# Expert jobs of 96 rows, with the weights held in the array in the up products

## The chip, the cores and the metric

One NeuronCore of a Trainium2 chip runs the whole program in one launch. The metric is device time in microseconds (us), the median of several executions. PE stands for TensorE's matmuls, PEld for its weight loads, DVE for VectorE, ACT for ScalarE, POOL for GpSimd and SP for SyncE, which here only issues transfers.

## The reference

A two-layer transformer over 256 tokens of width 1024, all float32. Each layer has a mixer (four kinds of token mixing, not touched here) and a feed-forward part. In the first layer that part is dense, in the second it is a mixture of eight experts, of which each token takes two:

```python
def swiglu(h, w1, w3, w2):
    return (jax.nn.silu(h @ w1) * (h @ w3)) @ w2

def moe_swiglu(h, w_router, w1, w3, w2):
    logits = (h @ w_router).astype(jnp.float32)
    top_v, top_i = lax.top_k(logits, TOP_K)                      # TOP_K = 2
    gates = jax.nn.softmax(top_v, axis=-1)
    combine = jnp.sum(jax.nn.one_hot(top_i, N_EXPERTS, ...) * gates[..., None], axis=-2)
    for e in range(N_EXPERTS):                                   # 8 experts, width 3584
        out = out + combine[..., e:e + 1] * swiglu(h, w1[e], w3[e], w2[e])
```

So 512 token rows are spread over eight experts. Counted by the reference's router on its own inputs, the experts get 53 to 78 rows each.

## The kernel before

The expert stage works through a list of jobs. A job is one expert and up to C = 128 of its token rows (`C = P`, L46); an expert with more rows than C would get a second job. There are eight jobs here. An expert's 3584 hidden columns are cut into 14 pairs of 256 columns, and each pair has three pieces of weights of 1 MB: two up pieces (w1 and w3 side by side, for the first and the second half of the 1024 inputs) and one down piece. So the stage has 112 pairs and 336 pieces.

SP fetches the pieces into a ring of seven slots (L1110). ACT rounds each piece to float32r (`wh`, L491), DVE takes the remainder (`wl`, L495), and `wh` and `wl` have four buffers each. Every product is made of three matmuls, high by high, high by low and low by high, all of float32r.

In `pe_up` (L402) the token rows are held in the array and the weights stream past them: 12 matmuls of 512 columns for each up piece (L417), 24 for a pair. Token rows then lie on PSUM's partitions, and w1's 256 columns and w3's lie side by side in one bank. ACT takes silu of the first half (L522), and DVE multiplies it with the second (`gate`, L577). The down product needs the hidden columns on partitions, so PE transposes the gated values (`pe_turn_gated`, L424, two transposes at L430), ACT rounds the result (`gh`, L535) and DVE takes the remainder (`gl`, L586). `pe_down` (L433) makes 12 matmuls of 512 columns (L442), again with the token values held in the array.

The order of PE is written out in `pe_steps` (L456): up half 0 of pair m, the transposes of pair m-1, up half 1 of pair m, down of pair m-1. ACT and DVE have their own written order, a round for each pair (L543 and L596): first the split of the gated values of pair m-1, then the up weights of pair m+1, silu and gate of pair m, and the down weights of pair m. Between two jobs PE also transposes the next rows (L854). In the dense layer the same functions hold the weights in the array and stream 256 columns of tokens past them (L420, L446).

Of the kernel before, what the change touches and what calls it, by code (L numbers as in the profile page):

```python
# [45 lines left out]
C = P  # L46
# [113 lines left out]
def program(nc, A, out):  # L160
    ctx = ExitStack()
    with ctx:
# [233 lines left out]
        TURNS = 4  # L396

# [4 lines left out]
        def pe_up(pe, run, m, par, part):  # L402
            stage, buf = run.up(m, part)
            pe.wait_ge(sem("w_split"), stage + 1)
            if part == 0:
                wait(pe, "gated", run.item(m - 1))
            w = [b[:, buf].rearrange("p (k n) -> p k n", n=2 * T) for b in (wh, wl)]
            for item in range(run.parts):
                for kind in range(1 if run.moe else 2):
                    for k in range(4):  # L410
                        for n, (a, b) in enumerate(((0, 0), (0, 1), (1, 0))):
                            x = (xh, xl)[a][:, 4 * part + k]

                            kw = {"start": part == kind == k == n == 0, "stop": part == 1 and k == 3 and n == 2,
                                  "skip_group_check": True}
                            if run.moe:
                                ins = nc.tensor.matmul(up_bank(run, par, 0)[:], x[:, 0:C], w[b][:, k], **kw)  # L417
                            else:
                                at = kind * T + item * P
                                ins = nc.tensor.matmul(up_bank(run, par, item)[:, kind * T:(kind + 1) * T],  # L420
                                                       w[b][:, k, at:at + P], x, **kw)
            ins.then_inc(sem("stage_used"), 1)

        def pe_turn_gated(pe, run, m):  # L424

            if run.moe:
                pe.wait_ge(sem("gated"), run.item(m) + 1)
                pe.wait_ge(sem("g_split"), run.before_pairs + m)
                for a in range(2):
                    ins = nc.tensor.transpose(bank[TURNS][:, a * P:(a + 1) * P], gate[:, 0, a * P:(a + 1) * P], cst("id"))  # L430
                ins.then_inc(sem("g_turned"), 1)

        def pe_down(pe, run, m, last=False, first=False, followed=False):  # L433
            stage, buf = run.down(m, last, followed)
            pe.wait_ge(sem("w_split"), stage + 1)
            pe.wait_ge(sem("g_split"), run.before_pairs + m + 1)
            w = [b[:, buf].rearrange("p (a n) -> p a n", a=2) for b in (wh, wl)]
            for o in range(2 if run.moe else KT):
                for a in range(2):
                    for g, b in ((gh, 0), (gh, 1), (gl, 0)):  # L440
                        if run.moe:
                            ins = nc.tensor.matmul(bank[2 + o][:], g[:, a, 0:C], w[b][:, a, o * 512:(o + 1) * 512],  # L442
                                                   start=first and a == 0 and g is gh and b == 0, stop=False,
                                                   skip_group_check=True)
                        else:
                            ins = nc.tensor.matmul(bank[2 + o // 2][:, o % 2 * T:(o % 2 + 1) * T],  # L446
                                                   w[b][:, a, o * P:(o + 1) * P], g[:, a],
                                                   start=first and o % 2 == a == b == 0 and g is gh, stop=False,
                                                   skip_group_check=True)
                if last and not run.moe and o % 2 and o < KT - 1:  # L450
                    ins.then_inc(sem("acc_ready"), 1)
                if last and run.moe and not followed and o == 0:
                    ins.then_inc(sem("acc_ready"), 1)
            ins.then_inc(sem("stage_used"), 1)

        def pe_steps(pe, run, j=0):  # L456

            def step(m, par, first=False):
                pe_up(pe, run, m, par, 0)
                pe_turn_gated(pe, run, m - 1)  # L460
                pe_up(pe, run, m, par, 1)
                if first and run.moe:
                    wait(pe, "acc_copied", 2 * j)
                pe_down(pe, run, m - 1, first=first)

            n = run.pairs - 1
            if run.moe:
                step(1, 1, True)
                with pe.Fori(0, n // 2) as i:
                    step(2 * i + 2, 0)  # L470
                    step(2 * i + 3, 1)
                return
            step(1, 1, True)
            with pe.Fori(0, (n - 1) // 2) as i:
                step(2 * i + 2, 0)
                step(2 * i + 3, 1)
            if n % 2 == 0:
                step(n, 0)
# [33 lines left out]

        def act_silu(act, run, m, par):
            for item in range(run.parts):
                if not run.moe:
                    act.wait_ge(sem("scaled"), run.item(m) + item + 1)
                    nc.scalar.activation(silu[:, item], silu[:, item], ACT.Silu, bias=cst("zero")
                                         ).then_inc(sem("silu_done"), 1)
                    continue
                act.wait_ge(sem("stage_used"), run.up(m, 1)[0] + 1)  # L520
                wait(act, "gated", run.item(m - 1) + item + 1)
                nc.scalar.activation(silu[:, item], up_bank(run, par, item)[:, 0:T], ACT.Silu, bias=cst("zero")  # L522
                                     ).then_inc(sem("silu_done"), 1)

        def act_gated_high(act, run, m):

            if run.moe:
                act.wait_ge(sem("g_turned"), run.before_pairs - PAIRS_D + m + 1)
                o, i = gh[:, :, 0:C], bank[TURNS][:, 0:2 * C].rearrange("p (a c) -> p a c", c=C)
            else:  # L530
                act.wait_ge(sem("gated"), run.item(m) + 2)
                o, i = gh[:], gate[:]
# [36 lines left out]
        def dve_gate(dve, run, m, par):  # L569
            for item in range(run.parts):  # L570
# [6 lines left out]
                nc.vector.tensor_tensor(gate[:, item], up_bank(run, par, item)[:, T:2 * T], silu[:, item], ALU.mult  # L577
                                        ).then_inc(sem("gated"), 1)

        def dve_gated_low(dve, run, m):  # L580
            dve.wait_ge(sem("g_high"), run.before_pairs + m + 1)
            if run.moe:
                o, i, h = gl[:, :, 0:C], bank[TURNS][:, 0:2 * C].rearrange("p (a c) -> p a c", c=C), gh[:, :, 0:C]
            else:
                o, i, h = gl[:], gate[:], gh[:]
# [10 lines left out]
        def dve_steps(dve, run):  # L596
            up, down = splitter(dve, split_low, run)

            for m in range(1, run.pairs - 1):
                dve_gated_low(dve, run, m - 1)  # L600
                up(m + 1, 0)
                if not run.moe:
                    dve_scale(dve, run, m, m % 2)
                    up(m + 1, 1)
                dve_gate(dve, run, m, m % 2)
                if run.moe:
                    up(m + 1, 1)
# [186 lines left out]
        def placed(tt=slice(0, TT)):  # L794
            return gh[:, tt, C:2 * C]

        def y_part(low, half):
            return (xh, xl)[low][:, 4 * half:4 * half + 4, C:2 * C]

        def acc_half(half):  # L800
            return bank[2 + half][:].rearrange("p (k c) -> p k c", c=C)
# [6 lines left out]
        def pe_moe(pe, mm, turn):  # L808
# [39 lines left out]
            def gather(j):  # L848

                pe.wait_ge(sem("x_loaded"), 16 * j)  # L850
                for half in range(2):
                    for d in range(4):
                        k = 4 * half + d
                        turn(bank[5 + half][:, d * C:(d + 1) * C], xrow[:, k * P:(k + 1) * P],  # L854
                             sig="gathered" if d == 3 else None)
# [11 lines left out]
            with pe.Fori(1, n_jobs) as j:  # L867
                run, nxt = job(j - 1), job(j, True)
                pe_turn_gated(pe, run, last)
# [9 lines left out]
            pe_turn_gated(pe, run, last)  # L879
            pe.wait_ge(sem("sel_built"), 2)  # L880
            for tt in range(TT):
                turn(bank[7][:, tt * P:(tt + 1) * P], sel[:, tt], sig="place_turned" if tt else None)
# [8 lines left out]
        def act_moe(act, copy, f):  # L891
# [9 lines left out]
            def gathered(j):  # L901
                for half in range(2):
                    act.wait_ge(sem("gathered"), 2 * j + half + 1)
                    nc.scalar.activation(xh[:, 4 * half:4 * half + 4, 0:C],
                                         bank[5 + half][:].rearrange("p (k c) -> p k c", c=C), ACT.Copy
                                         ).then_inc(sem("x_high"), 1)

            def acc(j):
                act.wait_ge(sem("stage_used"), job(j).used())
                act.wait_ge(sem("y_stored"), 16 * j + 16)  # L910
                for half in range(2):
                    nc.scalar.copy(yj[:, half * 512:(half + 1) * 512], bank[2 + half][:]).then_inc(sem("acc_copied"), 1)
# [23 lines left out]
            nc.scalar.activation(placed(), bank[7][:, 0:T].rearrange("p (a c) -> p a c", c=C), ACT.Copy).then_inc(sem("last_high"), 1)  # L936
# [13 lines left out]
        def dve_moe(dve, settle, tt_, ts, stt, recip):  # L950
# [44 lines left out]
            def gathered(j):  # L995
                for half in range(2):
                    dve.wait_ge(sem("x_high"), x_before(1, 2) + 2 * j + half + 1)
                    hv = slice(4 * half, 4 * half + 4)
                    nc.vector.tensor_tensor(xl[:, hv, 0:C], bank[5 + half][:].rearrange("p (k c) -> p k c", c=C),
# [3 lines left out]
            for i in range(2):  # L1003
                settle(nc.vector.tensor_tensor(hit[:, i], cst("iota").unsqueeze(1).broadcast_to([P, TT, C]),
# [17 lines left out]
            for i in range(2):  # L1022
                settle(nc.vector.tensor_tensor(hit[:, i], cst("iota").unsqueeze(1).broadcast_to([P, TT, C]),
# [43 lines left out]
        def pool_moe(pool, settle):  # L1067
# [9 lines left out]
            def load(j):  # L1077
                pool.dma_start(xrow[:], job_x[bass.ds(j * C, C), :]).then_inc(sem("x_loaded"), 16)

            def store(j):  # L1080
                pool.wait_ge(sem("acc_copied"), 2 * j + 2)
                pool.dma_start(job_y[bass.ds(j * C, C), :], yj[:]).then_inc(sem("y_stored"), 16)
# [98 lines left out]
        def _(pool):  # L1181
# [17 lines left out]
            for layer in range(DEPTH):  # L1199
# [50 lines left out]
                if layer == 0:  # L1250
                    settle(nc.gpsimd.memset(xrow[:], 0.0))
                    for rows_, sig in ((job_x, "zero_filled"), (job_y, "y_stored")):
                        pool.dma_start(rows_.rearrange("(j p) d -> p j d", p=C),
                                       xrow[:].unsqueeze(1).broadcast_to([P, MAXJOBS, D])).then_inc(sem(sig), 16)
# [1154 lines left out]
```

## Time and profile before

| | us |
|---|---|
| three runs | 1645.98, 1646.78, 1652.68 |
| median | 1646.78 |
| span of the profiled execution | 1645.5 |
| first up product of the experts in that execution | 672.4 |
| last down product done | about 1634 |

The profile is one execution. A page gives busy time by engine, the span in 40 slices, the chain that ended last and the costliest groups of instructions. The trace behind it gives the same for any stretch, and the instructions one by one. A matmul row's own duration is longer than the step to the next one, because matmuls are pipelined: what a stream of them costs is the step from start to start.

### The profile page before, as it was taken

The page shows a single profiled execution, that of the slowest core. Times are in us where ns is not written, and L with a number is a line of the kernel's source. Part 1 is how long each engine was busy: PE and PEld are TensorE (multiplying, and loading weights), DVE is VectorE, ACT ScalarE, POOL GpSimd, SP SyncE. Part 2 cuts the span into 40 slices and gives each one's busy share as a digit, 9 for nine tenths or more (in the row PEclk, how much of TensorE's full clock was granted, in tenths as well). Part 3 has the DMA queues.
Part 4 walks back from the last instruction along what each step waited for, and adds up shares of the span by engine and source line. Part 5 has one row for each costly group of instructions (what it writes and reads, how often), then busy time and mean ns, then how long its engine had stood idle before and what let it go on. Part 6 is the DMA issues. An engine that isn't in the chain of part 4 may idle for free.

```text
span 1645.5 us, 27766 instructions
## 1 busy us (share of the span) xinstructions
PE 1585.1 (96%) x10290; PEld 1363.3 (83%) x10290; DVE 1283.7 (78%) x1252; ACT 1041.8 (63%) x1038; POOL 139.9 (9%) x152
## 2 busy tenths in 40 slices
PE   7999989999899999899999999999999999999997
PEld 7987789999898778788888888888888888888776
DVE  4885556555558656688889889889888888988997
ACT  4634454344354445577777777777777777777675
POOL 1062000000006200100000000000000000001720
PEclk9999999999999999999999999999999999999999
DMA  7429165542252105699999999999999999999992
GB/s 252 159 89 398 55 256 184 186 170 99 80 176 88 40 2 225 247 374 375 382 375 374 389 375 377 382 374 384 378 375 361 399 373 367 395 373 369 398 356 111
DMA packets 68272, 457.56 MB, mean 278 GB/s; under 512 B 7296, under 2 KB 8480, under 8 KB 16752
## 3 DMA queue, kind: packets, MB, share of 16 engines
q1 hardware_dynamic: 59984, 425.80, 67.1%
q0 software_dynamic: 8080, 30.84, 4.9%
q8 instruction: 43, 0.70, 0.2%
q14 instruction: 21, 0.17, 0.0%
q10 hardware_dynamic: 144, 0.05, 0.0%
HBM read 433.07 MB, written 23.59 MB: 278 GB/s over the span
## 4 chain that ended last, share of the span: by engine, by line
PE 54%; issue 3%; DVE 3%; ACT 2%; DVEq 0%; ACTq 0%
PE bank L417 33%; PE bank L442 17%; DVE wl L495 2%; PE bank L430 1%; ACT wh L491 1%; PE bank L738 1%; PE bank L1271 1%; DVE gl L586 0%; PE bank L814 0%; PE bank L1276 0%; PE bank L483 0%; DVE gate L577 0%; ACT wide L1770 0%; ACT oh L728 0%; DVE rstd L2026 0%
## 5 line engine op out<-in xcount | busy, mean ns | idle before, releaser
L495 DVE TENSOR_TENSOR wl<-ring,wh 128x2048 fp32r<-128x2048 f32 x369 | 854.0, 2318 | 157.7 <-ACT wh L491 154.4
L491 ACT ACTIVATE wh<-ring 128x2048 fp32r<-128x2048 f32 x369 | 706.6, 1917 | 99.5 <-PE bank L442 46.9
L417 PE MATMUL bank<-wh,xh 128*128 128x512 f32 x896 | 358.0, 400 | 3.6 <-DVE wl L495 3.0
L417 PE MATMUL bank<-wh,xl 128*128 128x512 f32 x896 | 350.3, 391 | 0.0
L417 PE MATMUL bank<-wl,xh 128*128 128x512 f32 x896 | 349.6, 390 | 0.0
L417 PEld LDWEIGHTS bank<-wh,xh 128*128 128x128 f32 x896 | 168.3, 188 | 36.7 <-DVE wl L495 3.7
L417 PEld LDWEIGHTS bank<-wh,xl 128*128 128x128 f32 x896 | 168.2, 188 | 35.5
L417 PEld LDWEIGHTS bank<-wl,xh 128*128 128x128 f32 x896 | 168.7, 188 | 32.2
L442 PE MATMUL bank<-wh,gh 128*128 128x512 f32 x448 | 175.4, 392 | 6.3 <-DVE gl L586 6.3
L442 PE MATMUL bank<-wh,gl 128*128 128x512 f32 x448 | 174.4, 389 | 0.0
L442 PE MATMUL bank<-wl,gh 128*128 128x512 f32 x448 | 174.3, 389 | 0.0
L535 ACT ACTIVATE gh<-bank 128x256 fp32r<-128x256 f32 x112 | 43.0, 384 | 112.3 <-PE bank L430 112.2
L683 ACT ACTIVATE mh<-ring 128x1024 fp32r<-128x1024 f32 (+1 forms) x52 | 53.0, 1025 | 91.4 <-PE bank L702 91.2
L702 PE MATMUL bank<-xh,mh 128*128 128x256 f32 x336 | 99.3, 296 | 11.1 <-DVE xl L653 6.9
L689 DVE TENSOR_TENSOR ml<-ring,mh 128x1024 fp32r<-128x1024 f32 (+1 forms) x52 | 62.3, 1206 | 56.1 <-ACT mh L683 55.3
L442 PEld LDWEIGHTS bank<-wh,gh 128*128 128x128 f32 x448 | 84.1, 188 | 26.1 <-DVE gl L586 6.2
L420 PE MATMUL bank<-xh,wh 128*128 128x256 f32 x352 | 100.6, 286 | 4.5 <-DVE wl L495 4.5
L420 PE MATMUL bank<-xl,wh 128*128 128x256 f32 x352 | 100.3, 285 | 0.0
L420 PE MATMUL bank<-xh,wl 128*128 128x256 f32 x352 | 100.3, 285 | 0.0
L442 PEld LDWEIGHTS bank<-wh,gl 128*128 128x128 f32 x448 | 84.1, 188 | 17.6
L442 PEld LDWEIGHTS bank<-wl,gh 128*128 128x128 f32 x448 | 84.1, 188 | 17.2
L522 ACT ACTIVATE silu<-bank,const 128x256 f32<-128x256 f32 x112 | 53.4, 477 | 70.5 <-PE bank L417 70.5
(336 smaller groups left out, 2434.2 us busy)
## 6 DMA issues: line engine op xcount, KB each, us to landing
ring<-in_moe_w SPq DMA_DIRECT2D x336, 1024.0 KB, 5.0
ring<-in_ffn_w SPq DMA_DIRECT2D x33, 1024.0 KB, 4.8
ring<-in_w_in SPq DMA_DIRECT2D x24, 1024.0 KB, 4.9
ring<-in_w_out SPq DMA_DIRECT2D x8, 1024.0 KB, 4.8
job_x<-xrow POOLq DMA_DIRECT2D x1, 8192.0 KB, 27.3
job_y<-xrow POOLq DMA_DIRECT2D x1, 8192.0 KB, 47.7
xrow<-job_x POOLq DMA_DIRECT2D x7, 512.0 KB, 9.3
job_y<-yj POOLq DMA_DIRECT2D x7, 512.0 KB, 4.4
```

The lines of the kernel that those rows point to most:

```text
L417: ins = nc.tensor.matmul(up_bank(run, par, 0)[:], x[:, 0:C], w[b][:, k], **kw)
L420: ins = nc.tensor.matmul(up_bank(run, par, item)[:, kind * T:(kind + 1) * T], w[b][:, k, at:at + P], x, **kw)
L430: ins = nc.tensor.transpose(bank[TURNS][:, a * P:(a + 1) * P], gate[:, 0, a * P:(a + 1) * P], cst("id"))
L442: ins = nc.tensor.matmul(bank[2 + o][:], g[:, a, 0:C], w[b][:, a, o * 512:(o + 1) * 512], start=first and a == 0 and g is gh and b == 0, s ...
L491: nc.scalar.activation(wh[:, buf], flat_slot(slot), ACT.Copy).then_inc(sem("w_high"), 1)
L495: nc.vector.tensor_tensor(wl[:, buf], flat_slot(run.place(i)[0]), wh[:, buf].bitcast(F32), ALU.subtract).then_inc(sem("w_split"), 1)
L522: nc.scalar.activation(silu[:, item], up_bank(run, par, item)[:, 0:T], ACT.Silu, bias=cst("zero")).then_inc(sem("silu_done"), 1)
L535: nc.scalar.activation(o, i, ACT.Copy).then_inc(sem("g_high"), 1)
L683: nc.scalar.activation(mh[:, part, :, 0:n], unit_weights(u)[:, 4 * part:4 * part + 4, 0:n], ACT.Copy).then_inc(sem("unit_high"), 1)
L689: nc.vector.tensor_tensor(ml[:, part, :, 0:n], unit_weights(u)[:, 4 * part:4 * part + 4, 0:n], mh[:, part, :, 0:n].bitcast(F32), ALU.subtr ...
L702: ins = nc.tensor.matmul(o[:, c * T:(c + 1) * T], l, r, start=part == c == k == n == 0, stop=part == 1 and k == 3 and n == 2, skip_group_c ...
L738: ins = nc.tensor.matmul(o[:, c * T:(c + 1) * T], (oh, ol)[b][:, q % 2, i, c * P:(c + 1) * P], (xh, xl)[a][:, k], start=start and n == 0, ...
```

## The change

A job has at most 96 rows. In the experts' up product the weights are held in the array, 128 hidden columns at a time, and the 96 token rows stream past them: for each up piece two kinds (w1, w3) by two halves of the 256 columns by four blocks of inputs by three products, 48 matmuls of 96 columns, 96 for a pair. The result has the hidden columns on partitions, so the two transposes of a pair, their PSUM bank and their semaphore go. ACT's silu, DVE's gate and the split of the gated values run on 128 by 192 values, and the split reads `gate` from SBUF. It keeps its place at the head of the next round, behind the down weights. The down product holds 96 columns of token values in the array instead of 128. Rows and buffers of the jobs shrink from 128 to 96.

```diff
-C = P
+C = 96
...
-            for item in range(run.parts):
-                for kind in range(1 if run.moe else 2):
+            for item in range(2):
+                for kind in range(2):
+                    at = kind * T + item * P
+                    if run.moe:
+                        at_c = (2 * kind + item) * C
+                        o, first = up_bank(run, par, 0)[:, at_c:at_c + C], item == 0
+                    else:
+                        o, first = up_bank(run, par, item)[:, kind * T:(kind + 1) * T], True
                     for k in range(4):
                         for n, (a, b) in enumerate(((0, 0), (0, 1), (1, 0))):
-                            x = (xh, xl)[a][:, 4 * part + k]
...
-                                ins = nc.tensor.matmul(up_bank(run, par, 0)[:], x[:, 0:C], w[b][:, k], **kw)
...
+                            x = (xh, xl)[a][:, 4 * part + k, 0:C if run.moe else T]
+                            ins = nc.tensor.matmul(o, w[b][:, k, at:at + P], x, start=first and part == kind == k == n == 0,
+                                                   stop=part == 1 and k == 3 and n == 2, skip_group_check=True)
             ins.then_inc(sem("stage_used"), 1)
-
-        def pe_turn_gated(pe, run, m):
-
-            if run.moe:
-                pe.wait_ge(sem("gated"), run.item(m) + 1)
-                pe.wait_ge(sem("g_split"), run.before_pairs + m)
-                for a in range(2):
-                    ins = nc.tensor.transpose(bank[TURNS][:, a * P:(a + 1) * P], gate[:, 0, a * P:(a + 1) * P], cst("id"))
-                ins.then_inc(sem("g_turned"), 1)
...
-                            ins = nc.tensor.matmul(bank[2 + o][:], g[:, a, 0:C], w[b][:, a, o * 512:(o + 1) * 512],
+                            ins = nc.tensor.matmul(bank[2 + o][0:C], g[:, a, 0:C], w[b][:, a, o * 512:(o + 1) * 512],
...
                 pe_up(pe, run, m, par, 0)
-                pe_turn_gated(pe, run, m - 1)
                 pe_up(pe, run, m, par, 1)
...
-            if run.moe:
-                act.wait_ge(sem("g_turned"), run.before_pairs - PAIRS_D + m + 1)
-                o, i = gh[:, :, 0:C], bank[TURNS][:, 0:2 * C].rearrange("p (a c) -> p a c", c=C)
-            else:
-                act.wait_ge(sem("gated"), run.item(m) + 2)
-                o, i = gh[:], gate[:]
+            act.wait_ge(sem("gated"), run.item(m) + run.parts)
+            o, i = (gated(gh), gated(gate)) if run.moe else (gh[:], gate[:])
```

## Rows read from the trace of the kernel before

**Rows 1.** The page: span, busy time of PE, granted clock and transfers by slice.
```profile
span 1645.5 us, 27766 instructions
PE 1585.1 (96%) x10290; PEld 1363.3 (83%) x10290; DVE 1283.7 (78%) x1252; ACT 1041.8 (63%) x1038; POOL 139.9 (9%) x152
...
PEclk9999999999999999999999999999999999999999
DMA  7429165542252105699999999999999999999992
```

**Rows 2.** Busy time by stretch: stretch, its length, each engine, clock, transfers' share, GB/s.
```profile
1000.00:1100.00 100.00, 99.76 (x456) 82.15 (x455) 89.77 (x61) 76.44 (x62) 1.06 (x2) 1.00 0.96 380
```

**Rows 3.** Waits in 800 to 1600: engine, line, releaser, total us, times, longest.
```profile
ACT gh L535 <- PE bank L430: 93.0, 88, 2.5
...
PEld bank L442 <- DVE gl L586: 4.7, 7, 1.8
PEld bank L417 <- DVE wl L495: 3.7, 3, 1.3
```

**Rows 4.** Waits of the SP queue in the same stretch.
```profile
SPq L1110 <- DVE wl L495: 626.1, 274, 4.4
```

**Rows 5.** Chain that ended last, final pairs: start, length, engine, line, count.
```profile
1618.95 2.72 PE bank L442 x12
1621.67 2.72 PE bank L417 x12
1624.39 0.22 PE bank L430 x2
1624.61 2.75 PE bank L417 x12
```

**Rows 6.** PE one by one: start and duration, of 512 columns, then of 256.
```profile
1203.64 0.39 PE L417 MATMUL bank<-wh,xh 128*128 128x512 f32 x1
...
1205.00 0.39 PE L442 MATMUL bank<-wh,gh 128*128 128x512 f32 x1
...
507.07 0.28 PE L702 MATMUL bank<-xl,mh 128*128 128x256 f32 x1
...
508.85 0.28 PE L702 MATMUL bank<-xl,mh 128*128 128x256 f32 x1
```

**Rows 7.** Weight loads in time, first start and total us, of matmuls of 8 columns.
```profile
661.74 1.08 PEld L1271 LDWEIGHTS bank<-rt,const 128*128 128x128 f32 x9
...
649.80 0.97 PEld L814 LDWEIGHTS bank<-router,hT 128*128 128x128 f32 x8
```

**Rows 8.** Weight loads by line: shortest, median and longest duration in ns.
```profile
L420 PEld LDWEIGHTS bank<-xl,wh x352: 187/192/329, 230.6 to 413.8; 128*128 128x128 f32 x176
...
L814 PEld LDWEIGHTS bank<-router,hT x32: 186/333/333, 649.7 to 655.3; 128*128 128x128 f32 x32
...
L430 PEld LDWEIGHTS bank<-const,gate x224: 138/139/143, 680.5 to 1629.9; 128*128 128x128 f32 x112
...
L1276 PEld LDWEIGHTS bank<-const,hT x16: 224/230/370, 655.4 to 658.7; 128*128 128x128 f32 x16
```

**Rows 9.** Stretches around three places where the clock falls, columns as in rows 2.
```profile
432.20:437.70 5.50, 2.23 (x11) 1.62 (x9) 5.46 (x11) 2.49 (x3) 0.00 (x0) 1.00 0.00 0
...
439.10:442.50 3.40, 3.40 (x18) 3.40 (x18) 0.87 (x1) 0.20 (x1) 0.00 (x0) 0.50 0.00 0
...
480.70:482.70 2.00, 0.00 (x1) 0.00 (x0) 1.29 (x2) 2.00 (x3) 0.00 (x0) 1.00 0.44 86
...
483.40:486.90 3.50, 3.50 (x19) 3.50 (x19) 0.37 (x1) 0.00 (x0) 0.00 (x0) 0.51 0.43 180
...
650.70:661.00 10.30, 10.30 (x46) 9.94 (x46) 8.54 (x22) 2.65 (x5) 0.00 (x0) 0.50 0.84 331
```

**Rows 10.** Weight loads of matmuls of 8 columns at the lower clock, as rows 7.
```profile
650.87 3.96 PEld L814 LDWEIGHTS bank<-router,hT 128*128 128x128 f32 x18
```

**Rows 11.** PE in time: plain float32 matmuls of 256 columns, two records for each.
```profile
664.55 1.03 PE L483 MATMUL bank<-const 128*128 128x256 f32 x4
```

More of the change, by code:

```diff
@@ L394, in job @@
                        PAIRS_D + PAIRS_E * j, lambda s: before(3, s) + 3 * PAIRS_E // SLOTS * j, follows)
-        TURNS = 4
         def up_bank(run, par, item):
@@ L407, in pe_up @@
             w = [b[:, buf].rearrange("p (k n) -> p k n", n=2 * T) for b in (wh, wl)]
-            for item in range(run.parts):
-                for kind in range(1 if run.moe else 2):
+            for item in range(2):
[6 more added lines that the diff above has]
+                        o, first = up_bank(run, par, item)[:, kind * T:(kind + 1) * T], True
                     for k in range(4):
                         for n, (a, b) in enumerate(((0, 0), (0, 1), (1, 0))):
-                            x = (xh, xl)[a][:, 4 * part + k]
-                            kw = {"start": part == kind == k == n == 0, "stop": part == 1 and k == 3 and n == 2,
-                                  "skip_group_check": True}
-                            if run.moe:
-                                ins = nc.tensor.matmul(up_bank(run, par, 0)[:], x[:, 0:C], w[b][:, k], **kw)
-                            else:
-                                at = kind * T + item * P
-                                ins = nc.tensor.matmul(up_bank(run, par, item)[:, kind * T:(kind + 1) * T],
-                                                       w[b][:, k, at:at + P], x, **kw)
-            ins.then_inc(sem("stage_used"), 1)
-        def pe_turn_gated(pe, run, m):
-            if run.moe:
-                pe.wait_ge(sem("gated"), run.item(m) + 1)
-                pe.wait_ge(sem("g_split"), run.before_pairs + m)
-                for a in range(2):
-                    ins = nc.tensor.transpose(bank[TURNS][:, a * P:(a + 1) * P], gate[:, 0, a * P:(a + 1) * P], cst("id"))
-                ins.then_inc(sem("g_turned"), 1)
+                            x = (xh, xl)[a][:, 4 * part + k, 0:C if run.moe else T]
+                            ins = nc.tensor.matmul(o, w[b][:, k, at:at + P], x, start=first and part == kind == k == n == 0,
+                                                   stop=part == 1 and k == 3 and n == 2, skip_group_check=True)
+            ins.then_inc(sem("stage_used"), 1)
         def pe_down(pe, run, m, last=False, first=False, followed=False):
@@ L511, in act_split, with gated @@
             return splitter(act, split_high, run)
+        def gated(buf, at=0):
+            if len(buf.shape) == 3:
+                return buf[:, :, 0:C]
+            return buf[:, at:at + 2 * C].rearrange("p (a c) -> p a c", c=C)
         def act_silu(act, run, m, par):
@@ L521, in act_silu @@
                 wait(act, "gated", run.item(m - 1) + item + 1)
-                nc.scalar.activation(silu[:, item], up_bank(run, par, item)[:, 0:T], ACT.Silu, bias=cst("zero")
+                nc.scalar.activation(gated(silu), gated(up_bank(run, par, 0)), ACT.Silu, bias=cst("zero")
                                      ).then_inc(sem("silu_done"), 1)
         def act_gated_high(act, run, m):
-            if run.moe:
-                act.wait_ge(sem("g_turned"), run.before_pairs - PAIRS_D + m + 1)
-                o, i = gh[:, :, 0:C], bank[TURNS][:, 0:2 * C].rearrange("p (a c) -> p a c", c=C)
-            else:
-                act.wait_ge(sem("gated"), run.item(m) + 2)
-                o, i = gh[:], gate[:]
+            act.wait_ge(sem("gated"), run.item(m) + run.parts)
+            o, i = (gated(gh), gated(gate)) if run.moe else (gh[:], gate[:])
             prev = run.stages if isinstance(m, int) and m == 0 else run.down(m - 1)[0] + 1
@@ L576, in dve_gate @@
                 wait(dve, "g_split", run.before_pairs + m)
-                nc.vector.tensor_tensor(gate[:, item], up_bank(run, par, item)[:, T:2 * T], silu[:, item], ALU.mult
+                nc.vector.tensor_tensor(gated(gate), gated(up_bank(run, par, 0), 2 * C), gated(silu), ALU.mult
                                         ).then_inc(sem("gated"), 1)
@@ L581, in dve_gated_low @@
             dve.wait_ge(sem("g_high"), run.before_pairs + m + 1)
[L582 to L585, printed above, removed]
+            o, i, h = (gated(gl), gated(gate), gated(gh)) if run.moe else (gl[:], gate[:], gh[:])
             nc.vector.tensor_tensor(o, i, h.bitcast(F32), ALU.subtract).then_inc(sem("g_split"), 1)
@@ L601, in dve_steps @@
                 up(m + 1, 0)
-                if not run.moe:
+                if run.moe:
+                    dve_gate(dve, run, m, m % 2)
+                    up(m + 1, 1)
+                else:
                     dve_scale(dve, run, m, m % 2)
                     up(m + 1, 1)
-                dve_gate(dve, run, m, m % 2)
-                if run.moe:
-                    up(m + 1, 1)
+                    dve_gate(dve, run, m, m % 2)
                 down(m)
@@ L794, in placed @@
         def placed(tt=slice(0, TT)):
-            return gh[:, tt, C:2 * C]
+            return gh[0:C, tt, P:2 * P]
         def y_part(low, half):
-            return (xh, xl)[low][:, 4 * half:4 * half + 4, C:2 * C]
+            return (xh, xl)[low][0:C, 4 * half:4 * half + 4, P:2 * P]
         def acc_half(half):
-            return bank[2 + half][:].rearrange("p (k c) -> p k c", c=C)
+            return bank[2 + half][0:C].rearrange("p (k c) -> p k c", c=P)
         LAST_BANKS = ((5, 6), (0, 1))
@@ L853, in gather @@
                         k = 4 * half + d
-                        turn(bank[5 + half][:, d * C:(d + 1) * C], xrow[:, k * P:(k + 1) * P],
-                             sig="gathered" if d == 3 else None)
+                        turn(bank[5 + half][:, d * C:(d + 1) * C], xrow[0:C, k * P:(k + 1) * P], C,
+                             "gathered" if d == 3 else None)
             last = PAIRS_E - 1
@@ L868, in pe_moe @@
                 run, nxt = job(j - 1), job(j, True)
-                pe_turn_gated(pe, run, last)
                 gather(j)
@@ L878, in pe_moe @@
             run = job(j)
-            pe_turn_gated(pe, run, last)
             pe.wait_ge(sem("sel_built"), 2)
             for tt in range(TT):
-                turn(bank[7][:, tt * P:(tt + 1) * P], sel[:, tt], sig="place_turned" if tt else None)
+                turn(bank[7][0:C, tt * P:(tt + 1) * P], sel[:, tt], sig="place_turned" if tt else None)
             pe_down(pe, run, last, True)
@@ L904, in gathered @@
                     nc.scalar.activation(xh[:, 4 * half:4 * half + 4, 0:C],
-                                         bank[5 + half][:].rearrange("p (k c) -> p k c", c=C), ACT.Copy
+                                         bank[5 + half][:, 0:4 * C].rearrange("p (k c) -> p k c", c=C), ACT.Copy
                                          ).then_inc(sem("x_high"), 1)
@@ L911, in acc @@
                 for half in range(2):
-                    nc.scalar.copy(yj[:, half * 512:(half + 1) * 512], bank[2 + half][:]).then_inc(sem("acc_copied"), 1)
+                    nc.scalar.copy(yj[0:C, half * 512:(half + 1) * 512], bank[2 + half][0:C]).then_inc(sem("acc_copied"), 1)
             last = PAIRS_E - 1
@@ L935, in act_moe @@
             act.wait_ge(sem("place_turned"), 1)
-            nc.scalar.activation(placed(), bank[7][:, 0:T].rearrange("p (a c) -> p a c", c=C), ACT.Copy).then_inc(sem("last_high"), 1)
+            nc.scalar.activation(placed(), bank[7][0:C, 0:T].rearrange("p (a c) -> p a c", c=P), ACT.Copy).then_inc(sem("last_high"), 1)
             f(tiny[:], cst("zero"), ACT.Sqrt)
@@ L998, in gathered @@
                     hv = slice(4 * half, 4 * half + 4)
-                    nc.vector.tensor_tensor(xl[:, hv, 0:C], bank[5 + half][:].rearrange("p (k c) -> p k c", c=C),
+                    nc.vector.tensor_tensor(xl[:, hv, 0:C], bank[5 + half][:, 0:4 * C].rearrange("p (k c) -> p k c", c=C),
                                             xh[:, hv, 0:C].bitcast(F32), ALU.subtract).then_inc(sem("x_split"), 1)
@@ L1003, in dve_moe @@
             for i in range(2):
-                settle(nc.vector.tensor_tensor(hit[:, i], cst("iota").unsqueeze(1).broadcast_to([P, TT, C]),
+                settle(nc.vector.tensor_tensor(hit[:, i], cst("iota")[:, 0:C].unsqueeze(1).broadcast_to([P, TT, C]),
                                                choice("slot")[:, i].unsqueeze(2).broadcast_to([P, TT, C]), ALU.is_equal))
@@ L1022, in dve_moe @@
             for i in range(2):
-                settle(nc.vector.tensor_tensor(hit[:, i], cst("iota").unsqueeze(1).broadcast_to([P, TT, C]),
+                settle(nc.vector.tensor_tensor(hit[:, i], cst("iota")[:, 0:C].unsqueeze(1).broadcast_to([P, TT, C]),
                                                in_last[:, i].unsqueeze(2).broadcast_to([P, TT, C]), ALU.is_equal))
@@ L1077, in load @@
             def load(j):
-                pool.dma_start(xrow[:], job_x[bass.ds(j * C, C), :]).then_inc(sem("x_loaded"), 16)
+                pool.dma_start(xrow[0:C], job_x[bass.ds(j * C, C), :]).then_inc(sem("x_loaded"), 16)
             def store(j):
                 pool.wait_ge(sem("acc_copied"), 2 * j + 2)
-                pool.dma_start(job_y[bass.ds(j * C, C), :], yj[:]).then_inc(sem("y_stored"), 16)
+                pool.dma_start(job_y[bass.ds(j * C, C), :], yj[0:C]).then_inc(sem("y_stored"), 16)
             pool.dma_start(fin, A["final_norm"].rearrange("(a d) -> a d", a=1).broadcast_to([P, D])
@@ L1253, in _ @@
                         pool.dma_start(rows_.rearrange("(j p) d -> p j d", p=C),
-                                       xrow[:].unsqueeze(1).broadcast_to([P, MAXJOBS, D])).then_inc(sem(sig), 16)
+                                       xrow[0:C].unsqueeze(1).broadcast_to([C, MAXJOBS, D])).then_inc(sem(sig), 16)
                 settle(nc.gpsimd.memset(xft[H:P, :, 0:H], 0.0))
```

## The prediction

> **What bounds the kernel now.** I read the page first: PE is busy 96% of a span of 1645.5 us at the full granted clock, and transfers are near their limit only in the second half, which is the expert stage [rows 1]. In a stretch of 100 us there, PE is busy 99.76, DVE 89.8 and ACT 76.4, and the transfer share is 0.96 at 380 GB/s [rows 2]. Next the waits: in 800 us of that stage PE waited some 8 us for splits; ACT's 93 us of waiting for the transposes cost nothing, since PE was streaming meanwhile [rows 3]. SP waits 626 us for DVE to free ring slots, so the fetches follow PE's pace through the buffers [rows 4]. PE is the bound, with transfers 4% behind it and DVE 10%.
>
> The chain shows a pair as PE alone: 2.72 (up) + 0.22 (two transposes) + 2.75 (up) + 2.72 (down) = 8.41 us [rows 5]. In single records the step from one 512-column matmul to the next is 1.36/6 = 0.227 us, and with 256 columns it is 1.78/15 = 0.1187 us [rows 6]. So a column costs (0.227 - 0.1187)/256 = 0.42 ns, and each matmul some 11 ns besides. In both shapes the next weight load hides under the stream.
>
> **The change part by part.**
>
> *Up products, the main term.* They go from 24 matmuls of 512 columns to 96 of 96 columns in each pair. The columns streamed fall from 12,288 to 9,216, a quarter less, and that would be the gain if time went by columns. But weight loads rise from 24 to 96, and a load no longer has 213 ns of streaming over it but 96 x 0.42 = 40 ns. What a load costs by itself is seen where almost nothing is streamed: matmuls of 8 columns are (1.08 - 0.19)/8 = 0.111 us apart in one place and (0.97 - 0.19)/7 = 0.111 us in another, at the full clock [rows 7]. I use 0.1114. These are plain float32 loads, and the new ones are of float32r. No matmul of the trace shows the step of float32r at under 256 columns, so the durations have to decide: a float32r load lasts 192 ns at the full clock and 329 at half of it, a plain one 186 (shortest) and 333, but the load of a transpose only 139 and 230 [rows 8]. Halving the clock adds 137 and 147 ns to the first two and 91 to the third. I read that as two passes over 128 columns for float32 and float32r alike, and one for a transpose. So I take 0.1114 for the new step: 96 x 0.1114 = 10.69 us. Bounds for it: from below, two passes of 128 columns at 0.42 ns, 0.1075; from above, the 256-column step, 0.1187, where the same float32r load hides. The pair's up goes from 5.47 to 10.69, with 10.32 to 11.40 as bounds.
>
> *Transposes.* -0.22 us of PE in each pair [rows 5]; PE's waits for the gate go with them.
>
> *Down products.* Still 12 of 512 columns; the smaller stationary operand has its load hidden, so 2.72 stays.
>
> *ACT and DVE.* Silu, gate and the two split steps shrink by a quarter of their columns, and ACT no longer waits for PE's transposes in `gh`. On the path this is worth nothing while PE is the bound: DVE's 7.5 us of work for a pair (0.898 x 8.41) stand against 13.4 us of PE. If that cover were gone, that is if PE fell under 7.5, DVE would be the bound. The wait added in `gh` (on `gated` in place of the transposes) has the next up weights queued behind it on ACT, and DVE's `gl` behind that. But the gate of pair m-1 is made a whole down split earlier, and `pe_down` needs `gl` only after two up pieces of 5.3 us. Nothing comes late from that.
>
> *Transfers and jobs.* 3.15 MB for a pair in 13.4 us is 235 GB/s against 380 now, so transfers drop behind. POOL's row loads and stores and the zero filling get smaller, beside other work. The experts have at most 78 rows, so 96 still makes eight jobs; between jobs PE turns 96 rows instead of 128, worth nothing that counts.
>
> *Sum.* A pair: 10.69 + 2.72 = 13.41 us against 8.41, +5.00; times 112 pairs +560 us. About 3 us of the waits for splits vanish, as PE leaves DVE and ACT more time. The span becomes 1645.5 + 560 - 3 = 2202. The median of the runs lies 1.3 us above the profiled span, which gives 2204 us. By the bounds of the step a pair takes 13.04 or 14.12 us, so this case alone reaches from 2163 to 2284.
>
> **The rivals.**
>
> *The clock falls in the up stretches.* Today PE streams almost all the time in the expert stage and the clock is full throughout. The falls in the trace come right after PE had been short of work, for example in a stretch of 5.5 us in which it was busy 2.2, or a gap of 2 us, and another time it stayed at half for 10.3 us although PE's records fill the stretch; the first 4 us of that were matmuls of 8 columns, bound by their loads, and they ran at half clock to their end [rows 9, 10]. The new up stretches are between these rows: 40 ns of streaming in every 111. Against it: the load is also followed by a wide stream here, and the down products stream fully each round. At half clock a load-bound step is (3.96 - 0.33)/17 = 0.2135 us [rows 10]. With half of each up stretch at that level, 96 x 0.1625 = 15.6, and the down at 2.72 to twice that, a pair takes 18.3 to 21.0 us: +1110 to +1410, so 2755 to 3060, the middle 2907. All of it at half clock: 20.5 + 5.4 = 25.9, 3610.
>
> *Narrow float32r streams are slower in themselves.* No row has float32r under 256 columns. If they ran as plain float32 does, a matmul of 256 columns costs two steps of (1.03 - 0.38)/3 = 0.217 us, 1.69 ns a column [rows 11], and 96 columns cost 0.162 + 0.011: 16.6 + 2.7 = 19.3 for a pair, 2870; with a load for both records (0.223) 24.1, 3405.
>
> *The float32r load is cheaper than two passes.* With one pass, as for the transposes, 50 ns less [rows 8]: 0.061 a step, 5.9 + 2.72 = 8.6 us, 1668. Half way, 0.086, 11.0 us for a pair, 1934. Against it stand the equal durations of the plain and the float32r load. (The Trainium skill, "TensorE: Matmul & The Clock Gate", section "Back-to-back issue gap", gives about 81 ns for sustained load-and-multiply pairs of 128 columns, which would make 7.8 + 2.7 = 10.5 us and 1880; but for 512 columns it gives 131, where this trace has 227, so I don't lean on it.)
>
> *Faster: the load hides entirely.* Then a step is 40 + 11 = 51 ns, PE needs 4.9 + 2.72 = 7.6 us, and the transfers, at a share of 0.96, become the bound at 8.07 us for a pair: -0.34 x 112 = -38, so 1609. It decides from the step at which the pairs break even, (8.41 - 2.72)/96 = 59 ns: any step below that is a gain, and the weight loads are nearly twice as far apart [rows 7]. (The same section of the Trainium skill has N/2.4 + 2.5 ns as the gap of isolated matmuls, 42.5 ns here, which would give this case; the measured 111 ns contradicts it where every step has a load [rows 7].)
>
> An expert of over 96 rows would add a job; the reference's draw rules that out as far as I see (0.01).
>
> **How the numbers follow.** Load-bound at the full clock 0.57; the clock falls 0.20; narrow streams slow 0.08; a cheaper load, slower all the same, 0.08; faster 0.04; the rest, among it an extra job or no change, 0.03. The prediction is the first, 2204, with 2163 to 2284 as its own range. To hold 8 in 10 the range has to take in most of the clock's case and the nearer part of the narrow streams: 0.57 + 0.18 + 0.05 = 0.80, from 2160 to 3060. It leaves out the cheaper load and the gain. What a measurement can tell from no change is about 0.5%, 8 us: slower by more 0.95, faster by more 0.04, the same 0.01.
>
> **What would show it.** Right: up matmuls some 111 ns apart, weight loads back to back over the whole up stretch, 10.7 us of up and 2.7 of down in a pair, the clock at 1.0, DVE near 55%, transfers near 235 GB/s, and no transposes in the chain. The clock's case: 0.5 in the clock row and steps of 213 ns. Narrow streams: steps of over 160 ns at full clock, with idle time between the loads. Wrong altogether: up steps under 60 ns with transfers at 0.96 or above.

## The result, and the profile after

The changed kernel takes 2935.8 us, the median of four runs (2923.3 to 2937.3), against 1646.5 us for the kernel before (here the median of four runs, one more than listed above): a ratio of 1.779, 95% interval 1.774 to 1.784. The time lies inside the stated range, but the case that I held likeliest gave 2204. What happened is the first rival, the falling clock, which I had priced at 2907 and given a chance of 0.20. The range holds the time only because it took this rival in; the sum itself is 732 us short.

The page of the kernel after: its span, PE's busy time, the granted clock and the transfers' share in 40 slices.

```profile
span 2935.7 us, 43224 instructions
PE 2877.9 (98%) x18130; PEld 2662.9 (91%) x18130; DVE 1271.4 (43%) x1253; ACT 1029.3 (35%) x1038; POOL 124.3 (4%) x152
...
PEclk9999999996666666666666666666666666666666
DMA  5436533114444444444444444444444444445440
```

PE is busier than before [rows 1], 98%. From the tenth slice on, where the expert stage begins, the clock is at 0.6 to 0.7 in every slice. Below stand the same stretch of 100 us as in [rows 2], in which DVE and transfers have fallen to less than half, then a low and a full part in the middle of a job, and the same where one job ends and the next begins (stretch, its length, busy time of PE, PEld, DVE, ACT, POOL, clock, transfers' share, GB/s):

```profile
1000.00:1100.00 100.00, 100.00 (x551) 91.84 (x551) 37.88 (x26) 33.36 (x27) 0.00 (x0) 0.67 0.45 158
...
1465.60:1479.10 13.50, 13.50 (x55) 12.08 (x55) 4.43 (x3) 3.85 (x3) 0.00 (x0) 0.50 0.41 150
1479.20:1486.00 6.80, 6.80 (x61) 6.68 (x59) 2.97 (x3) 3.03 (x3) 0.00 (x0) 1.00 0.55 173
...
1503.10:1520.10 17.00, 17.00 (x73) 15.84 (x73) 5.79 (x5) 2.83 (x4) 0.00 (x0) 0.50 0.32 129
1520.10:1527.00 6.90, 6.71 (x45) 5.39 (x43) 3.67 (x4) 4.88 (x6) 0.00 (x0) 1.00 0.39 152
```

A mean of 0.67 is a mixture of the two levels, 1.2 and 2.4 GHz: in the middle of a job 13.5 us at half, then 6.8 at full; at the change of job 17 at half, then 7 at full, in which two down products stand with the turning of the next rows between them. PE's records leave no idle time in the low parts. The single records show both levels in one up stretch, the last of a job (start, duration, line, operands):

```profile
1499.90 0.27 PE L418 MATMUL bank<-xh,wl 128*128 128x96 f32 x1
...
1502.92 0.27 PE L418 MATMUL bank<-xh,wl 128*128 128x96 f32 x1
1503.03 0.37 PE L418 MATMUL bank<-xl,wh 128*128 128x96 f32 x1
1503.20 0.41 PE L418 MATMUL bank<-xh,wh 128*128 128x96 f32 x1
...
1516.43 0.41 PE L418 MATMUL bank<-xl,wh 128*128 128x96 f32 x1
1516.64 0.70 PE L431 MATMUL bank<-wh,gh 128*96 128x512 f32 x1
```

From 1499.90 to 1502.92 there are 27 steps of 3.02/27 = 0.112 us, the load-bound step of [rows 7]. From 1503.20 to 1516.43 there are 62 steps of 13.23/62 = 0.2134 us, the load-bound step at half clock of [rows 10]. Of all such steps in the expert stage that lie away from a change of the clock, 4876 are at the full clock, with a median of 0.112 us, and 4853 at half, with 0.213. The weight loads alone, in the full-clock part, follow each other without a pause, some 0.111 us from start to start:

```profile
1500.08 0.19 PEld L418 LDWEIGHTS bank<-xh,wh 128*128 128x128 f32 x1
1500.19 0.19 PEld L418 LDWEIGHTS bank<-xh,wl 128*128 128x128 f32 x1
1500.31 0.19 PEld L418 LDWEIGHTS bank<-xl,wh 128*128 128x128 f32 x1
```

The chain (start, length, engine, line, count) shows what [rows 5] showed, PE alone, without the transposes. Two pairs here, the second the last of its job, take 14.58 + 5.20 and 17.25 + 4.41 us, where a pair took 8.41. Below them stand the second down at the change of job and the two ups at the head of the next job, which have no down between them:

```profile
1479.81 14.58 PE bank L418 x96
1494.39 5.20 PE bank L431 x12
1499.59 17.25 PE bank L418 x96
1516.84 4.41 PE bank L431 x12
...
1522.08 3.01 PE bank L431 x12
1525.09 35.89 PE bank L418 x192
1560.98 4.50 PE bank L431 x12
```

The waits from 800 to 2900 us have ACT waiting for PE and DVE for ACT. Those of the weight loads, against [rows 3], are down to 2.6 us, seven times (engine, line, releaser, total, times, longest):

```profile
ACT silu L516 <- PE bank L418: 820.9, 105, 8.3
DVE gate L567 <- ACT silu L516: 652.3, 105, 11.0
...
PEld bank L431 <- DVE gl L573: 2.6, 7, 0.4
```

### The profile page after: what moved, and what is told of

It is laid out like the page before. It is cut to its first block, busy times and chain, and to the rows that moved or that the text cites. A ratio compares the mean times of both kernels' runs of the same rounds, so it can differ in the third digit from the quotient of the medians.

```text
span 2935.7 us, 43224 instructions
## 1 busy us (share of the span) xinstructions
PE 2877.9 (98%) x18130; PEld 2662.9 (91%) x18130; DVE 1271.4 (43%) x1253; ACT 1029.3 (35%) x1038; POOL 124.3 (4%) x152
## 4 chain that ended last, share of the span: by engine, by line
PE 77%; DVE 0%; ACT 0%; issue 0%; DVEq 0%; ACTq 0%
PE bank L418 59%; PE bank L431 17%; PE bank L726 0%; PE bank L1257 0%; PE bank L802 0%; PE bank L1262 0%; PE bank L471 0%; ACT gh L525 0%; DVE gl L573 0%; ACT wide L1756 0%; ACT oh L716 0%; DVE rstd L2012 0%; DVE wide L2009 0%; DVE ol L722 0%; PE bank L874 0%
## 5 line engine op out<-in xcount | busy, mean ns | idle before, releaser
L418 PE MATMUL bank<-xl,wh 128*128 128x96 f32 (+1 forms) x3936 | 1332.3, 338 | 0.0
L418 PE MATMUL bank<-xh,wl 128*128 128x96 f32 (+1 forms) x3936 | 1328.4, 337 | 0.0
L418 PE MATMUL bank<-xh,wh 128*128 128x96 f32 (+1 forms) x3936 | 1317.7, 335 | 5.0 <-DVE wl L483 4.5
L418 PEld LDWEIGHTS bank<-xh,wh 128*128 128x128 f32 x3936 | 1002.8, 255 | 14.6 <-issue 5.5
L418 PEld LDWEIGHTS bank<-xh,wl 128*128 128x128 f32 x3936 | 1007.3, 256 | 5.1
L418 PEld LDWEIGHTS bank<-xl,wh 128*128 128x128 f32 x3936 | 1011.1, 257 | 0.0
L431 PE MATMUL bank<-wh,gh 128*96 128x512 f32 x448 | 261.4, 584 | 1.9 <-DVE gl L573 1.9
L431 PE MATMUL bank<-wl,gh 128*96 128x512 f32 x448 | 248.7, 555 | 0.0
L431 PE MATMUL bank<-wh,gl 128*96 128x512 f32 x448 | 235.3, 525 | 0.0
L431 PEld LDWEIGHTS bank<-wh,gh 128*96 128x96 f32 x448 | 114.4, 255 | 49.4 <-DVE gl L573 3.5
```

The costliest lines, as they stand in the source:

```text
L418: ins = nc.tensor.matmul(o, w[b][:, k, at:at + P], x, start=first and part == kind == k == n == 0, stop=part == 1 and k == 3 and n == 2, s ...
L431: ins = nc.tensor.matmul(bank[2 + o][0:C], g[:, a, 0:C], w[b][:, a, o * 512:(o + 1) * 512], start=first and a == 0 and g is gh and b == 0, ...
```

## The experiments

Three things had to be told apart: what the loads cost at the full clock, what the clock added, and why it fell. The runs with useless matmuls, with half the columns and with two products are single ones; the four runs of the changed kernel lie within 14 us, so differences of hundreds of us stand clear of that.

### 128 rows again

```diff
-C = 96
+C = P
```

> The changed kernel with jobs of 128 rows again, and nothing else undone: the same 96 weight loads for a pair, but 128 columns streamed behind each, 53 ns instead of 40 by the column price of 0.42 ns. Theory A (a step is bound by its weight load, 0.111 us at the full clock, and the clock falls because so little is streamed between the loads): the load still covers the wider stream, the clock holds at 1.0, a pair takes 96 x 0.1114 + 2.72 = 13.4 us, and the time is 2204 us, some 730 less than with 96 rows, although a third more columns are streamed. Rival B (the clock falls because of the loads themselves, however wide the stream): the clock stays near 0.66 in the expert stage and the time near 2936. Rival C (narrow streams are slow in themselves, by columns): the up products take a third longer, over 3300.

It took 2211.1 us, 1.341 times before (1.338 to 1.344). Its stretch and its chain:

```profile
1300.00:1400.00 100.00, 100.00 (x808) 96.32 (x807) 56.27 (x38) 46.80 (x36) 0.00 (x0) 1.00 0.65 240
...
1310.61 10.67 PE bank L418 x96
1321.28 2.83 PE bank L431 x12
```

Theory A is right to 7 us, and the clock is at 1.00 over the whole expert stage. A third more columns are streamed, and the kernel is 725 us faster than with 96. The loads are as many and the step is the same, 10.67/96 = 0.111 us, so the loads alone are not what makes the clock fall; the streaming between them has a part in it. This run also cuts the loss in two: 561 us (2211 - 1650, the kernel before on the same chip) for the change at the full clock, the loads above all, and 725 us for the clock; the step at the full clock is the same with 96 columns, 0.112 us.

### Useless matmuls added

```diff
+                    if run.moe:
+                        nc.tensor.matmul(bank[4][0:C], xh[:, 4 * part, 0:C], w[0][:, 0], start=True, stop=True,
+                                         skip_group_check=True)
                     for k in range(4):
```

> The changed kernel (96 rows) with work added: ahead of each 12 up matmuls of a block, one more matmul of 512 columns into a PSUM bank that nobody reads, 8 for a pair. Theory A (too little streamed between the loads lets the clock fall): if 8 are enough the clock holds and a pair takes 13.4 + 8 x 0.227 = 15.2 us, 2410 us in all, some 520 less with more work; if they are not enough, the clock keeps falling and the time lies between 2700 and 3200. Rival B (the loads themselves make it fall): the added matmuls cost 8 x 0.23 to 0.43 us a pair, 3140 to 3320 us.

It took 2389.1 us: with 896 matmuls more, 547 us less than the changed kernel. The jobs have 96 rows and the up products are untouched. The clock is back, and in the chain the block of 12 loads is at its full-clock length, 1.27 us from the filler's end:

```profile
1300.00:1400.00 100.00, 99.82 (x766) 91.81 (x765) 46.91 (x34) 41.80 (x36) 1.01 (x2) 1.00 0.59 216
...
1314.27 0.27 PE bank L415
1314.54 1.27 PE bank L421 x12
```

A block is 0.27 + 1.27 = 1.54 us, eight of them 12.3, and with 2.8 for the down a pair is 15.1, against the 15.2 expected. So neither the row count nor the loads force the low clock, and the down, which holds 96 columns here and 128 in the run before, is not its cause either.

### Half the columns

```diff
-                        o, first = up_bank(run, par, 0)[:, at_c:at_c + C], item == 0
+                        o, first = up_bank(run, par, 0)[:, at_c:at_c + C // 2], item == 0
...
-                            x = (xh, xl)[a][:, 4 * part + k, 0:C if run.moe else T]
+                            x = (xh, xl)[a][:, 4 * part + k, 0:C // 2 if run.moe else T]
```

> The changed kernel with half of each job's columns left out of the up products: 48 columns streamed behind each load instead of 96, loads and everything else unchanged (so half of the up results are missing). Theory A: the step stays 0.111 us at the full clock and 0.2135 at half, since the load sets it, and the clock is low at least as often: 2930 to 3610 us. Rival C (time by columns): the up stretches halve, -5 us or more for a pair, under 2400 us.

It took 3133.6 us, 198 more than with 96 columns, though half of the streaming is gone. Its clock is 0.60 over the expert stage against 0.66, and in a stretch of 100 us:

```profile
1300.00:1400.00 100.00, 100.00 (x512) 94.35 (x512) 33.12 (x23) 29.55 (x24) 0.00 (x0) 0.61 0.41 145
...
1299.82 0.39 PE L418 MATMUL bank<-xl,wh 128*128 128x48 f32 x1
1300.04 0.39 PE L418 MATMUL bank<-xh,wh 128*128 128x48 f32 x1
1300.25 0.39 PE L418 MATMUL bank<-xh,wl 128*128 128x48 f32 x1
```

The step at half clock is 0.43/2 = 0.215 us, over the whole stage 0.213 in the median, and 0.112 at full, as with 96 columns. Time by columns (rival C) is out: with 96 columns or fewer the step is the load's, and taking columns away only costs clock.

### One product of three left out

```diff
-C = 96
+C = P
...
                         for n, (a, b) in enumerate(((0, 0), (0, 1), (1, 0))):
+                            if run.moe and n == 1:
+                                continue
```

> As e1_128rows (128 columns behind each load, clock at 1.0 there, 13.4 us a pair), with one of the three products left out of the experts' up products (high by low), so 64 weight loads for a pair in place of 96; everything else, the splits too, as there. Theory A (time goes by the number of loads, 0.1114 us each at the full clock): 64 x 0.1114 + 2.72 = 9.85 us a pair, 3.6 less, 2211 - 399 = 1812 us. Rival D (something else than the loads sets the pair, such as the splits on ACT and DVE with their 7.5 us, the ring or the waits between stages): a pair takes clearly more than 9.85 us and PE waits for splits; the time is over 1900 us.

It took 1817.9 us against 1812 expected. The chain:

```profile
1306.18 7.10 PE bank L420 x64
1313.27 2.83 PE bank L433 x12
```

7.10/64 = 0.111 us a load again, and 9.93 us a pair, 0.08 over the sum. At the full clock, and with 128 columns behind each load, the up products go by the number of loads; the splits, with DVE busy 76.29 of 100 us, do not bound the pair.

### 96 rows, weights streaming as before

```diff
+            if run.moe:
+                for k in range(4):
+                    for n, (a, b) in enumerate(((0, 0), (0, 1), (1, 0))):
+                        ins = nc.tensor.matmul(up_bank(run, par, 0)[0:C], (xh, xl)[a][:, 4 * part + k, 0:C], w[b][:, k],
...
+                for a in range(2):
+                    ins = nc.tensor.transpose(bank[TURNS][:, a * C:(a + 1) * C], gate[0:C, 0, a * P:(a + 1) * P],
+                                              cst("id")[0:C, 0:C])
...
```

> Only the row count of the change: jobs of 96 rows, but the weights stream past the token rows as before (24 up matmuls of 512 columns, transposes kept, of 96 rows now). Theory A: the row count costs nothing; steps of 0.227 us, clock 1.0, and the two transposes of a pair stream 96 columns instead of 128 at 0.107/128 us a column, 0.05 us less for a pair: 6 us less, 1640. Rival: smaller jobs are part of the loss (loads of 96 columns, buffers, rows), more than 1660 us.

It took 1654.4 us in the median of twelve runs, 1.0033 times before (1.0016 to 1.0051). The row count is no part of the large loss, as expected, but it isn't the 6 us gain either: it is some 4 us slower. The chain and a load row (shortest, median, longest ns):

```profile
1410.80 2.76 PE bank L409 x12
1413.56 0.17 PE bank L438 x2
1413.72 2.77 PE bank L409 x12
1416.49 2.76 PE bank L451 x12
...
L409 PEld LDWEIGHTS bank<-wh,xh x896: 159/161/163, 676.8 to 1633.5; 128*96 128x96 f32 x180
```

The transposes did fall from 0.22 [rows 5] to 0.17 us. But 12 matmuls of 512 columns take 2.76 us where they took 2.72, though the load of 96 columns is shorter, 161 ns, than that of 128. Two such groups, and the one behind the transposes with 2.77 against 2.75, make +0.1 us a pair, twice what the transposes give.

### The same, with 128 columns held in the array

Against the run before it; the last 32 columns of the down's token values are set to zero.

```diff
-                        ins = nc.tensor.matmul(up_bank(run, par, 0)[0:C], (xh, xl)[a][:, 4 * part + k, 0:C], w[b][:, k],
+                        ins = nc.tensor.matmul(up_bank(run, par, 0)[:], (xh, xl)[a][:, 4 * part + k, 0:P], w[b][:, k],
...
-                            ins = nc.tensor.matmul(bank[2 + o][0:C], g[:, a, 0:C], w[b][:, a, o * 512:(o + 1) * 512],
+                            ins = nc.tensor.matmul(bank[2 + o][:], g[:, a, 0:P], w[b][:, a, o * 512:(o + 1) * 512],
...
```

> As e3_96_streamed (jobs of 96 rows, the weights streaming as before), but the operand held in the array has 128 columns again, the last 32 of them without meaning; transposes still of 96 rows. In e3_96_streamed the steps were 2.76/12 = 0.230 us against 0.227 before, and its time 0.3% above before's. Theory E (a held operand of 96 columns makes each step 3 ns longer): the step returns to 0.227, a pair takes 36 x 0.227 + 0.17 = 8.33 us against 8.41, and the time falls to some 8 us under before, a ratio of 0.995. Rival F (the 3 ns come from the jobs or the row count otherwise): steps of 0.230 stay, the ratio stays at 1.003.

It took 1645.0 us against 1650.1 for the kernel before on the same chip, a ratio of 0.998 (0.996 to 1.000). The chain and a load row:

```profile
1306.37 2.72 PE bank L409 x12
1309.09 0.17 PE bank L438 x2
1309.26 2.77 PE bank L409 x12
1312.03 2.72 PE bank L451 x12
...
L409 PEld LDWEIGHTS bank<-wh,xh x896: 186/188/189, 671.6 to 1621.4; 128*128 128x128 f32 x180
```

Two of the three groups are back at 2.72, so theory E holds: the narrower held operand makes the stream's steps longer, by which mechanism no run shows. The group behind the transposes stays at 2.77, against 2.75 before [rows 5]: its last steps are back at 0.227 us too, but its first one takes 0.31, where it took 0.29 with 96 columns. So a pair is 8.38 us and not 8.33, which makes some 3 us less than before in all. The gain is 5 us where 8 were expected, with an interval that all but touches none. It is the only version here under the time of before.

## Why the prediction was wrong

**The step of the up products: right.** I took 0.1114 us for a float32r load from plain float32 rows and from equal durations. The changed kernel has 0.112 at the full clock and 0.2134 at half, against the 0.2135 of [rows 10]. Narrow streams are not slow in themselves, and the float32r load is not cheaper than the plain one [rows 7]: both rivals are gone by the same records.

**Transposes, waits, transfers, jobs: right, and worth nothing on the path.** The transposes are gone from the chain, the loads wait 2.6 us in all for the gated values, there are eight jobs, and SP, POOL, ACT and DVE are beside PE's work. The new place of the gated split never comes late within a job; the seven waits are one for each change of job. DVE is at 38% and transfers at 158 GB/s, not the 55% and 235 that I named, because the pair is longer still; with 128 rows, at the full clock, they are 56% and 240.

**The sum at the full clock: right, for another kernel.** With 128 columns the clock holds, and 2211 us stand where I had worked out 2204. What is off there is the down, 2.83 us instead of 2.72.

**What failed: the clock term, taken at zero.** The sum has the up stretches at the full clock throughout; the runs showed a mean of 0.66 over the expert stage, and 725 us for it. The likeliest case carried the full clock over from a kernel that streams nearly all the time. I had the rows that spoke against it [rows 9, 10] and set against them that here a wide stream follows each load and the down products stream fully each round. Neither kept the clock: the down gave it back, as in 1479.2 to 1486.0, and the next up stretch lost it again. The expert stage has 104 up stretches, and in each of them the clock fell once, after 33 to 60 loads. It rose 104 times, 96 of them inside a down and 8 within 0.5 us after one. At the head of each job, where two ups of 96 loads stand together, it stayed low for 34 us, until the down behind them. The price of the rival was right: it put half of the up at the lower level, as measured, and 18.3 to 21.0 us for a pair; the first down begins at 721.1 us and the last, 111 pairs on, at 2921.5, which makes 19.8 us a pair, and 2907 stood against 2936. The wrong thing was the order of the two chances, 0.57 and 0.20. The trace of before had no stretch of loads with 40 ns of streaming behind each, so it could not decide; with rows on both sides and none for this case, setting the two near even would have been sounder.

The Trainium skill ("TensorE: Matmul & The Clock Gate", section "Why this matters for your kernels") says to avoid drops by leaving no long idle gaps between bursts of matmuls. This case bounds that advice: PE shows 100.00 us busy of 100 with the clock at 0.67. Busy records are not streaming, though: by the prediction's 0.42 ns a column the 96 columns fill 40 ns of a step of 111. The same page of the Trainium skill, section "LDWEIGHTS (loading the stationary operand)", gives the load's time by its columns, which makes an estimate of 107 ns for 128; the trace agrees within 5 ns at the full clock, but at half clock it shows 213.

**What stays open.** The run with 128 rows and the one with useless matmuls both add columns to the stream, the one to every step, the other in eight wide bursts a pair. No run tells whether the total or the spacing matters, and none lies between 96 and 128 columns. Spreading the 12 down products evenly between the loads of the up products would put wide streams into every stretch without added work. No run shows whether that keeps the clock, or whether the buffers for the split weights suffice for it.

## What to carry to other kernels

Count weight loads before columns: with float32r operands a new load of 128 columns for each matmul cost 0.111 us here at the full clock. By the prediction's 11 ns a matmul and 0.42 ns a column that is an estimated 240 columns of stream ((111 - 11)/0.42); with fewer behind each load the loads set the time, as 48, 96 and 128 columns showed. When the streaming behind the loads gets thin, check the granted clock too, since a PE that is busy all the time can run at half of it; here that cost more (725 us) than the loads (561). A kernel in which less work takes longer, or more work takes less, is a sign of it.

## What the runs showed of the hardware that I had not expected

- With the same 96 loads a pair, 128 columns behind each kept the clock at 1.00 over the expert stage, 96 gave a mean of 0.66 and 48 gave 0.60. Eight added matmuls of 512 columns a pair brought the 96-column kernel back to 1.00.
- A held operand of 96 columns loads faster (161 ns against 188), but a stream of 512-column matmuls over it steps 0.230 us instead of 0.227. Filling it up to 128 with columns that mean nothing takes the 3 ns back.
- Twelve down matmuls that follow narrow, load-bound ones take 2.83 us instead of 2.72.
